# Block attention of the odd layer: as a stage after its input projection, or woven into it by quarter tiles

## The chip, the cores and the metric

The kernel runs on one core of one Trainium2 chip. The metric is the device time of one execution in microseconds (us); the runs of a kernel are summarised by their median. TensorE (PE in the rows, PEld its weight loads), VectorE (DVE), ScalarE (ACT), GpSimd (POOL) and SyncE (SP) each work through a queue of their own in order and wait for one another through semaphores.

## The reference: what is computed

One inference step of a two-layer decoder trunk for a prompt of 256 tokens and 8 samples of 8 new tokens (320 tokens in all, model width 2048, float32). Layer 0 mixes with a state-space scan and a short convolution, layer 1 with block-sparse attention; after each comes a cross-attention into 256 memory tokens, at the end a norm. The part at issue is layer 1:

```
q, k, v, g = split(rmsnorm(x) @ w_in)        # 16 q heads, 4 kv heads of 128, gate of 2048
prompt:  p = softmax(q.k * scale - slope * distance, causal);  o = p.v
sample:  past = 2048 tokens = 8 blocks of 256, in 16 pages of 128 tokens found by page_table
         gate = q . mean of a block's keys; the top 3 of 8 blocks, and the own new tokens, are kept
         p = softmax over the kept keys (with -slope * distance);  o = p.v
x = x + (o * silu(g)) @ w_out
```

## The kernel before

Activations lie transposed: 128 channels in the partitions, 320 tokens in the free dimension, 16 chunks `k`. A projection (`Proj`) is a list of output tiles of 128 channels. For each tile a weight block of 1 MB (`load`, issued on SP, rows of 512 bytes) is split into a rounded part (`high`, ScalarE, L120) and a rest (`low`, VectorE, L125), and `Proj.tile` issues 48 matmuls with 320 columns: per chunk the rounded weights with the rounded and the rest part of the activations (L164), then the rest weights (L168). Four weight buffers are loaded ahead (`RAW`), three rounded ones are kept (`HI`). Tiles rotate over four PSUM banks, or two where `banks=(0, 1)` is given.

`moba` runs layer 1's attention in stages, each closed by a barrier of all engines:
- the projection `p_od`: 40 tiles, 16 of q, 4 of k, 4 of v, 16 of the gate; VectorE evacuates each into `m_q`, `m_k`, `m_v`, `m_g`, ScalarE applies SiLU to the gate;
- six transposed copies of k and v (`m_krows`, `m_vrows`) that are stored;
- `prompt_attention`: per head scores (L1650), bias and maximum on VectorE, exponentials on ScalarE (L1686), turns (transposes on TensorE against an identity, L1672), values (L1663). The scores are computed for the whole 256 x 256 square;
- `moba_sample`: a hardware loop over 8 samples. SP loads 16 key pages per sample (256 KB, rows of 2 KB, address read from the page table with `value_load`), GpSimd the value pages (both L1861). TensorE turns each key page in 4 pieces (L1937) into two alternating banks, ScalarE copies them out (L2014). Then scores (L1943), biasing and block sums and maxima (L2053 to L2056), the ranking of blocks (a chain of small VectorE operations), nine exponentials (L2026), turns of the probabilities (L1956), values (L1970), a scaled output and its turn (L2001);
- `residual_block` for the output projection `p_odo`: it first splits the gated output into two parts (L2220, L2234) and then runs 16 tiles, adding each to the residual stream `xt`.

In the even layer another order exists already: the steps of its scan (such as L1027, L1039, L1047) stand between whole tiles of the projection `p_sc`.

Of the kernel before, what the change touches and what calls it, by code (L numbers as in the profile page):

```python
# [12 lines left out]
ds = bass.ds  # L13
# [33 lines left out]
def host_constants():  # L47
# [19 lines left out]
    head, tok = np.arange(128) // TS, np.arange(128) % TS  # L67
    past = (-slopes[head][:, None] * (PAST + tok[:, None] - np.arange(PAST)[None]).astype(f)).astype(f)
    col = np.arange(64)
    own = np.full((128, NB, 64), NEG, f)  # L70
    for b in range(NB):
        d = tok[:, None] - (col[None] - TS * b)
        ok = (col[None] // TS == b) & (d >= 0)
        own[:, b] = np.where(ok, -slopes[head][:, None] * d.astype(f), f(NEG))
# [3 lines left out]
    return {"c_main": c, "c_dist": dist, "c_past": past, "c_own": own.reshape(128, 512),  # L78
# [50 lines left out]
class Proj:  # L129
# [19 lines left out]
    def tile(self, pe, t, rhs, ready=None):  # L149
# [10 lines left out]
        for k in range(self.kch):  # L160
            if ready:
                ready(pe, k)
            for part in range(2):
                e.nc.tensor.matmul(out, hi[:, k, cols], rhs(k)[part], start=(k == 0 and part == 0), stop=False)  # L164
        if t % self.tps == 0:
# [3 lines left out]
        m.then_inc(e.pe_tile, 1)  # L169
# [1672 lines left out]
class Pages:  # L1842


    QUAD = 4

    def __init__(self, e, ctx):
        self.e = e
        self.s = ctx.enter_context(stage(e.nc, "pages", ["pages_in"] + [f"{k}_in{i}" for k in "kv" for i in range(NPG // self.QUAD)]))
        self.table = e.at("page_table", 82, [1, NB * NPG], I32)  # L1850
        self.krows = e.at("key_pages", 84, [128, NPG, 512])
        self.vrows = e.at("value_pages", 28, [128, NPG, 512])

    def load(self, eng, kind, b, g, free=None):

        src = self.e.d[f"cache_{kind}"][0].rearrange("n t h c -> n t (h c)")
        dst = self.krows if kind == "k" else self.vrows
        page = eng.value_load(self.table[0:1, ds(b * NPG + g, 1)], min_val=0, max_val=src.shape[0] - 1)
        if free:
            eng.wait_ge(*free)  # L1860
        eng.dma_start(dst[:, g:g + 1, :], src[ds(page, 1)].rearrange("n t c -> t n c")).then_inc(self.s[f"{kind}_in{g // self.QUAD}"], 16)  # L1861

    def first(self, sp):

        sp.dma_start(self.table[:], self.e.d["page_table"].rearrange("b n -> (b n)").unsqueeze(0)).then_inc(self.s["pages_in"], 16)
        sp.wait_ge(self.s["pages_in"], 16)
        for g in range(NPG):
            self.load(sp, "k", 0, g)


def moba_sample(e, pages, qt, kt_new, v_new, gt, nxt):

    nc, d = e.nc, e.d
    names = ["zeroed", "tables_in", "q_ready", "k_turned", "kt_out", "scores", "own_scores", "step", "biases",
             "exped", "recips", "p_turned", "pt_v", "pt_s", "v_used", "o_ready", "o_rows", "o_turned", "o_out"]
    QUAD, HALF = Pages.QUAD, NPG // 2
    with ExitStack() as ctx:
        s = ctx.enter_context(stage(nc, "ms", names))
        NP = PAST + TSA
        past, own = e.at("ms_past", 116, [128, PAST]), e.at("ms_own", 76.75, [128, NB, TSA])  # L1890
        krows, vrows = pages.krows, pages.vrows
        kt = e.at("ms_kt", 175, [128, KVH, PAST])
        p, pt = e.at("ms_p", 60, [128, NP]), e.at("ms_pt", 68.25, [128, (NPG + 1) * 128])
        orows = e.at("ms_orows", 78.75, [128, DH])
        above, tied = [e.at(f"ms_{n}", 79.25 + 0.25 * i, [128, NBLK, NBLK]) for i, n in enumerate(("above", "tied"))]
        qb = e.at("ms_q", 79.75, [128, AH, TS])
        gate, rank, drop, top, dropped, bias, den, nm, den1, rec = [
            e.at(f"ms_{n}", 80.25 + 0.0625 * i, [128, w]) for i, (n, w) in enumerate(
                (("gate", NBLK), ("rank", NBLK), ("drop", NBLK + 1), ("top", NBLK + 1), ("dropped", NBLK + 1), ("bias", NBLK + 1),
                 ("den", NBLK + 1), ("negmax", 1), ("den_sum", 1), ("rec", 1)))]  # L1900
        STEPS = 25
        with nc.Block() as block:
            @block.sync
            def _(sp):
                sp.dma_start(past[:], d["c_past"]).then_inc(s["tables_in"], 16)
                sp.dma_start(own[:], d["c_own"].rearrange("p (b t) -> p b t", b=NB)).then_inc(s["tables_in"], 16)
                with sp.Fori(0, NB - 1) as b:
                    for g in range(NPG):

                        pages.load(sp, "k", b + 1, g, (s["k_turned"], b * NPG + (NPG + g + 1)))  # L1910

                sp.wait_ge(s["v_used"], NPG + NB * NPG)
                for n in range(nxt.slot0, nxt.slot0 + RAW):
                    e.load(sp, n)

            @block.gpsimd
            def _(pool):
                with pool.Fori(0, NB) as b:
                    for g in range(NPG):

                        pages.load(pool, "v", b, g, (s["v_used"], b * NPG + (g + 1)))

            @block.tensor
            def _(pe):
                mm = nc.tensor.matmul
                pe.sem_inc(s["k_turned"], NPG)
                pe.sem_inc(s["v_used"], NPG)

                def turn(b, g):
                    if g % QUAD == 0:  # L1930

                        pe.wait_ge(pages.s[f"k_in{g // QUAD}"], b * 64 + 64)
                    if g >= 2 or not isinstance(b, int):

                        pe.wait_ge(s["kt_out"], b * NPG + (g - 1))
                    for h in range(KVH):
                        m = nc.tensor.transpose(e.bank[g % 2][:, 128 * h:128 * h + 128], krows[:, g, 128 * h:128 * h + 128], e.ident)  # L1937
                    m.then_inc(s["k_turned"], 1)

                def scores(b, q):  # L1940
                    pe.wait_ge(s["kt_out"], b * NPG + QUAD * (q + 1))
                    for h in range(KVH):
                        m = mm(e.bank[4 + q][32 * h:32 * h + 32, :], qb[:, 4 * h:4 * h + 4, :].rearrange("p g t -> p (g t)"),  # L1943
                               kt[:, h, 512 * q:512 * q + 512], start=True, stop=True)
                    m.then_inc(s["scores"], 1)

                def first_scores(b):
                    pe.wait_ge(s["q_ready"], b + 1)
                    scores(b, 0)
                    scores(b, 1)  # L1950

                def turn_probs(b, f):

                    pe.wait_ge(s["exped"], b * 9 + (2 * f + 3))
                    for a in range(4):
                        m = nc.tensor.transpose(e.bank[4 + f][:, 128 * a:128 * a + 128], p[:, 512 * f + 128 * a:512 * f + 128 * a + 128], e.ident)  # L1956
                    m.then_inc(s["p_turned"], 1)
                    if f == 0:
                        nc.tensor.transpose(e.bank[3][0:TSA, 0:128], p[:, PAST:NP], e.ident).then_inc(s["p_turned"], 1)

                def values(b, f):

                    if f < 3:
                        pe.wait_ge(s["pt_v"], b * 4 + (f + 2 if f else 1))
                    else:
                        pe.wait_ge(s["pt_s"], b + 1)
                    pe.wait_ge(pages.s[f"v_in{f}"], b * 64 + 64)
                    for g in range(QUAD * f, QUAD * f + QUAD):
                        for h in range(KVH):
                            m = mm(e.bank[2][32 * h:32 * h + 32, 128:256], pt[:, 128 * g + 32 * h:128 * g + 32 * h + 32],  # L1970
                                   vrows[:, g, 128 * h:128 * h + 128], start=g == 0, stop=False, skip_group_check=True)
                        m.then_inc(s["v_used"], 1)

                def batch(b, last):
                    for g in range(HALF, NPG):
                        turn(b, g)
                        if g % QUAD == QUAD - 1:
                            scores(b, g // QUAD)
                    for h in range(KVH):
# [3 lines left out]
                    if not last:  # L1983
                        for g in range(HALF):
                            turn(b + 1, g)
# [475 lines left out]
```

## Time and profile before

| what | us |
|---|---|
| median of 3 runs (lowest, highest) | 2281.72 (2277.15, 2282.34) |
| profiled execution, its own time | 2278.83 |
| span of the profile, first to last instruction | 2277.2 |
| TensorE busy | 2099.7 |
| VectorE busy | 1186.1 |
| ScalarE busy | 914.8 |

The profile is of one execution. Busy time counts instructions in flight; matmuls overlap, so the mean duration of one is longer than the distance from one to the next. The granted clock is TensorE's, as a share of full speed. "Idle before" is what an engine waited just ahead of an instruction, and behind the arrow stands what ended that wait.

### The profile page before, as it was taken

How to read it: one execution, taken by the hardware profiler on the slowest of the kernel's cores; microseconds unless marked ns; L12 is line 12 of the kernel's file. 1: busy time of each engine (PE TensorE's matmuls, PEld its weight loads, DVE VectorE, ACT ScalarE, POOL GpSimd, SP SyncE). 2: the span in 40 equal slices, each digit the busy share in tenths (PEclk: the TensorE clock that was granted, in tenths of full speed). 3: DMA queues.
4: the chain of work that ended last, by engine and by line, in shares of the span. 5: the costliest groups of instructions: out<-in, count | busy, mean ns of one | idle time of the engine just before them, and what ended most of it. 6: DMA issues, size and time to landing. Idle time of an engine off the chain costs nothing. (4 is left out here: it accounts for less than half of the span.)

```text
span 2277.2 us, 39583 instructions
## 1 busy us (share of the span) xinstructions
PE 2099.7 (92%) x15842; PEld 1972.9 (87%) x15842; DVE 1186.1 (52%) x1819; ACT 914.8 (40%) x1426; POOL 146.1 (6%) x247
## 2 busy tenths in 40 slices
PE   7999999999999999999999878999977878599976
PEld 6899999999999999999999868999965555499956
DVE  5658666464554644565454346333326555445335
ACT  7445544243342523454333234223325555333322
POOL 1010000101101010001000000000000333100000
PEclk9999999999999999999999989999989999799988
DMA  8585455655656556555555714555523998555711
GB/s 236 173 216 154 132 148 129 166 136 151 170 130 167 135 157 190 149 149 146 151 151 162 230 43 128 150 149 148 148 80 126 353 339 284 145 150 164 234 67 47
DMA packets 516776, 369.05 MB, mean 162 GB/s; under 512 B 10699, under 2 KB 469624, under 8 KB 515882
## 3 DMA queue, kind: packets, MB, share of 16 engines
q1 hardware_dynamic: 498498, 305.47, 47.8%
q0 software_dynamic: 18128, 61.43, 8.3%
q8 instruction: 113, 1.85, 0.3%
q14 instruction: 37, 0.30, 0.0%
HBM read 348.29 MB, written 18.57 MB: 161 GB/s over the span
## 5 line engine op out<-in xcount | busy, mean ns | idle before, releaser
L120 ACT ACTIVATE w_high<-w_raw 128x2048 fp32r<-128x2048 f32 x232 | 443.9, 1913 | 895.0 <-PE bank L168 827.6
L125 DVE TENSOR_TENSOR w_low<-w_raw,w_high 128x2048 fp32r<-128x2048 f32 x232 | 531.4, 2290 | 268.2 <-ACT w_high L120 268.0
L164 PE MATMUL bank<-x_hi,w_high 128*128 128x320 f32 x1664 | 495.1, 312 | 0.0
L164 PE MATMUL bank<-x_lo,w_high 128*128 128x320 f32 x1664 | 489.5, 309 | 0.0
L164 PEld LDWEIGHTS bank<-x_hi,w_high 128*128 128x128 f32 x1664 | 312.4, 188 | 1.1
L164 PEld LDWEIGHTS bank<-x_lo,w_high 128*128 128x128 f32 x1664 | 312.5, 188 | 0.2
L168 PE MATMUL bank<-x_hi,w_low 128*128 128x320 f32 x1664 | 260.9, 309 | 0.0
L168 PEld LDWEIGHTS bank<-x_hi,w_low 128*128 128x128 f32 x1664 | 248.3, 188 | 0.0
L164 PE MATMUL bank<-xo_x_hi,w_high 128*128 128x320 f32 x640 | 189.9, 311 | 8.3 <-PEq L102 8.3
L164 PE MATMUL bank<-xo_x_lo,w_high 128*128 128x320 f32 x640 | 189.4, 310 | 0.0
L164 PEld LDWEIGHTS bank<-xo_x_hi,w_high 128*128 128x128 f32 x640 | 121.1, 189 | 8.6 <-issue 8.5
L164 PEld LDWEIGHTS bank<-xo_x_lo,w_high 128*128 128x128 f32 x640 | 121.1, 189 | 0.1
L168 PE MATMUL bank<-xo_x_hi,w_low 128*128 128x320 f32 x640 | 100.4, 309 | 0.0
L2014 ACT ACTIVATE ms_kt<-bank 128x512 f32<-128x512 f32 x128 | 69.8, 595 | 73.2 <-PE bank L1937 73.1
L168 PEld LDWEIGHTS bank<-xo_x_hi,w_low 128*128 128x128 f32 x640 | 95.5, 188 | 0.0
L164 PE MATMUL bank<-m_o_hi,w_high 128*128 128x320 f32 x256 | 78.6, 321 | 15.4 <-DVE m_o_lo L2234 15.4
L1349 DVE TENSOR_TENSOR xt<-xt,bank 128x320 f32<-128x320 f32 x80 | 38.8, 485 | 103.1 <-PE bank L168 103.1
L1937 PEld LDWEIGHTS bank<-const,key_pages 128*128 128x128 f32 x512 | 55.7, 143 | 31.9 <-ACT ms_kt L2014 18.2
L1937 PE MATMUL bank<-const,key_pages 128*128 128x128 f32 x512 | 73.0, 287 | 11.0 <-ACT ms_kt L2014 8.6
L1861 POOL DMA_DIRECT2D value_pages<-in_cache_v x128 | 68.8, 538 | 197.7 <-issue 136.7
L164 PE MATMUL bank<-m_o_lo,w_high 128*128 128x320 f32 x256 | 78.1, 319 | 0.0
L164 PE MATMUL bank<-ysc_hi,w_high 128*128 128x320 f32 x256 | 76.3, 313 | 0.0
(417 smaller groups left out, 3511.5 us busy)
## 6 DMA issues: line engine op xcount, KB each, us to landing
w_raw<-in_ev_w_in SPq DMA_DIRECT2D x104, 1024.0 KB, 5.8
w_raw<-in_od_w_in SPq DMA_DIRECT2D x40, 1024.0 KB, 5.7
w_raw<-in_ev_w_out SPq DMA_DIRECT2D x32, 1024.0 KB, 5.8
key_pages<-in_cache_k SPq DMA_DIRECT2D x128, 256.0 KB, 4.6
value_pages<-in_cache_v POOLq DMA_DIRECT2D x128, 256.0 KB, 4.6
w_raw<-in_ca_w_kv SPq DMA_DIRECT2D x16, 1024.0 KB, 7.3
w_raw<-in_ca_w_q SPq DMA_DIRECT2D x16, 1024.0 KB, 5.6
w_raw<-in_od_w_out SPq DMA_DIRECT2D x16, 1024.0 KB, 5.9
```

Of the source, the lines that this page charges most:

```text
L120: self.nc.scalar.activation(self.w_high[n % HI][:], self.w_raw[n % RAW][:], ACT.Copy).then_inc(self.w_hi, 1)
L125: self.nc.vector.tensor_tensor(self.w_low[n % RAW][:], self.w_raw[n % RAW][:], self.w_high[n % HI][:].bitcast(F32), ALU.subtract).then_inc ...
L164: e.nc.tensor.matmul(out, hi[:, k, cols], rhs(k)[part], start=(k == 0 and part == 0), stop=False)
L168: m = e.nc.tensor.matmul(out, lo[:, k, cols], rhs(k)[0], start=False, stop=k == self.kch - 1)
L1349: e.nc.vector.tensor_tensor(e.xt[:, t, :], e.xt[:, t, :], p.bank(t)[:, 0:T], ALU.add).then_inc(e.bank_free, 1)
L1861: eng.dma_start(dst[:, g:g + 1, :], src[ds(page, 1)].rearrange("n t c -> t n c")).then_inc(self.s[f"{kind}_in{g // self.QUAD}"], 16)
L1937: m = nc.tensor.transpose(e.bank[g % 2][:, 128 * h:128 * h + 128], krows[:, g, 128 * h:128 * h + 128], e.ident)
L2014: nc.scalar.activation(kt[:, :, 128 * g:128 * g + 128], e.bank[g % 2][:].rearrange("p (h t) -> p h t", h=KVH), ACT.Copy).then_inc(s["kt_ou ...
```

## The change

The stages of layer 1 up to the output projection become one block without barriers (`moba_layer`, class `Moba`). `Proj.tile` becomes a generator `parts` that yields after each matmul. Each of the 40 tiles is cut into four quarters of 12 matmuls; `weave` puts the attention's steps of a quarter between equal runs of these matmuls. `steps(qr)` gives the steps of quarter `qr` from a written-out timetable, and ScalarE and VectorE go through the same timetable.

- The order of tiles is k0, k1, q0 to q7, v0, v1, k2, k3, q8 to q15, v2, v3, gate. Projections use banks 0 and 1; bank 2 holds sample scores, 3 to 5 are turn-over banks (`TN`), 6 sample outputs, 7 prompt scores.
- The samples are done in 8 units `U`, each of two samples and two kv heads, 12 quarters apart from quarter 40 on. A unit has four groups (`Q`, three quarters apart): key turns (`K`, two steps of 8 turns), scores (`S`) two quarters after, turns of probabilities (`T`) at 16 and values (`V`) at 19 quarters. A page DMA now moves half a page (two of the four kv heads: 128 rows of 1 KB, 128 KB), 512 of them instead of 256; two groups of pages fit into each ring. Indices are written out instead of computed in a loop.
- Probabilities lie in five chunks of 512 columns; the distance bias is made from one row of key numbers and a per-row slope, its constant part added to the block's bias.
- One prompt head goes with each tile of 11 to 18 and 23 to 30 (`pS`, `pT`, `pO`); its fully masked quarter is left out.
- The gate is `x * (1 + tanh(x/2)) / 2` instead of SiLU: a tanh on ScalarE and two operations on VectorE.
- New tiles lie where `xt` lay, so `xt` is written to DRAM at the start and read back at the end. The splits for the output projection begin during the last tiles.

```diff
-class Pages: ...
-def moba_sample(e, pages, qt, kt_new, v_new, gt, nxt): ...
-def moba(e, p_in, p_out, res_in): ...
+class Moba:
+    BASE0, PERIOD = 40, 12
+    SC, TN, MI, PR = 2, (3, 4, 5), 6, 7
+    TAIL, CHUNKS = 14, 5
...
+    def steps(self, qr):
+        j, qi = divmod(qr, 4)
+        if qi == 1 and j and 16 <= self.order[j - 1] < 24:
+            yield "rows", j - 1, 0
+        for U in self.rel(qr, 31):
+            yield "OT", U, 0
...
+            for U in self.rel(qr, 19 + 3 * a):
+                yield "V", U, a
...
+            for U in self.rel(qr, 16 + 3 * a):
+                yield "T", U, a
...
+            for U in self.rel(qr, 2 + 3 * a):
+                yield "S", U, a
...
+            for U in self.rel(qr, 3 * a):
+                yield "K", 4 * U + a, 0
+                yield "K", 4 * U + a, 1
+        if qi == 0:
+            for h in self.head(j - 1):
+                yield "pT", h, 0
+            for h in self.head(j):
+                yield "pS", h, 0
...
+    def page(self, eng, kind, Q, bi, free):
...
+        for g in range(4):
+            page = eng.value_load(self.table[0:1, ds(b * NPG + 4 * q + g, 1)], min_val=0, max_val=src.shape[0] - 1)
+            if g == 0 and free:
+                eng.wait_ge(*free)
+            eng.dma_start(dst[c % 4][:, g:g + 1, :], src[ds(page, 1), :, 256 * hp:256 * hp + 256].rearrange("n t c -> t n c")).then_inc(sem[c % 4], 16)
...
+    def sync(self, sp):
...
+            if qr % 4 == 0 and qr:
+                e.load(sp, m + qr // 4 - 1 + RAW)
...
+                if qr == self.BASE0 + 3 * Q + 1:
+                    for bi in range(2):
+                        self.page(sp, "k", Q + 2, bi, (s["turned"], self.fill[("K", Q, bi), 1] + 1))
...
+    def pool(self, pool):
...
+            for bi in range(2):
+                self.page(pool, "v", Q, bi, (s["v_used"], Q - 1) if Q >= 2 else None)
+        self.out_of(pool, ("OT", 7, 0))
+        pool.wait_ge(s["p_probs"], AH)
+        pool.dma_start(e.xt[:].rearrange("p c t -> p (c t)"), e.spill).then_inc(s["xt_in"], 16)
...
+    def turn_bank(self, pe, key, f=0):
+        i = self.fill[key, f]
+        if i >= 3:
+            pe.wait_ge(self.s["turn_out"], i - 2)
+        return self.e.bank[self.TN[i % 3]]
...
+    def gate_scalar(self, act, h):
...
+        e.nc.scalar.activation(self.th[h % 2][:], self.tb[h % 2][:], ACT.Tanh, scale=0.5).then_inc(s["tanh"], 1)
...
+def weave(pe, parts, steps, run):
+    count = 12 // (len(steps) + 1)
+    for step in steps:
+        for _ in range(count):
+            next(parts)
+        run(pe, step)
+    for _ in range(12 - count * len(steps)):
+        next(parts, None)
+
+def moba_layer(e, p_in, p_out, res_in):
...
+            for j in range(n):
+                parts = p_in.parts(pe, j, res_in.rhs, res_in.ready if j == 0 else None)
+                for qi in range(4):
+                    weave(pe, parts, list(b.steps(4 * j + qi)), b.tensor)
...
+                    if qi == 2:
+                        e.high(act, m + j + AHEAD)
...
+                    for step in b.steps(qr):
+                        b.scalar(act, step)
+                    for U in b.rel(qr, 13):
+                        b.exps(act, U)
...
-        p_od = Proj(e, columns(d["od_w_in"][0], wide(0, 40)))
-        p_odo = Proj(e, columns(d["od_w_out"][0], wide(0, 16)))
+        p_od = Proj(e, columns(d["od_w_in"][0], [128 * n for n in (16, 17, *range(8), 20, 21, 18, 19, *range(8, 16), 22, 23, *range(24, 40))]), banks=(0, 1))
+        p_odo = Proj(e, columns(d["od_w_out"][0], wide(0, 16)), banks=(0, 1))
...
-        res = moba(e, p_od, p_odo, res)
+        res = moba_layer(e, p_od, p_odo, res)
```

## Rows read from the trace of the kernel before

**Rows 1.** The page's busy times: engine, us, share of the span, instructions.

```profile
PE 2099.7 (92%) x15842; PEld 1972.9 (87%) x15842; DVE 1186.1 (52%) x1819; ACT 914.8 (40%) x1426; POOL 146.1 (6%) x247
```

**Rows 2.** Windows: stretch, length; PE, PEld, DVE, ACT, POOL busy; clock, DMA share, GB/s.

```profile
1395.60:1679.40 283.80, 283.80 (x1922) 283.50 (x1922) 108.72 (x79) 81.44 (x56) 0.00 (x0) 0.99 0.48 134
1679.40:1696.30 16.90, 2.93 (x25) 2.58 (x25) 2.56 (x4) 2.27 (x5) 2.56 (x4) 0.69 0.29 94
1696.30:1749.80 53.50, 41.66 (x192) 29.37 (x192) 39.43 (x96) 28.31 (x81) 0.00 (x0) 0.97 0.28 79
1749.80:1963.40 213.60, 170.15 (x2064) 113.47 (x2064) 107.71 (x273) 108.78 (x280) 68.82 (x128) 0.93 0.87 302
...
1779.00:1805.00 26.00, 21.26 (x262) 13.97 (x266) 13.43 (x35) 13.54 (x35) 9.01 (x17) 0.94 1.01 366
396.73:443.33 46.60, 46.60 (x385) 45.02 (x381) 22.87 (x41) 12.85 (x14) 7.52 (x10) 1.00 0.64 167
```

**Rows 3.** Timeline of layer 1: start us, us, instruction, idle before it.

```profile
1395.58 0.61 PE L164 MATMUL bank<-xo_x_hi,w_high 128*128 128x320 f32 x1 [8.29 <-PEq L102]
...
1975.88 0.60 PE L164 MATMUL bank<-m_o_hi,w_high 128*128 128x320 f32 x1 [12.89 <-DVE m_o_lo L2234]
...
1990.95 0.31 PE L164 MATMUL bank<-m_o_hi,w_high 128*128 128x320 f32 x1
```

**Rows 4.** Line L113, weight loads: plain tiles, woven even tiles; ns, first and last start.

```profile
L113 SPq DMA_DIRECT2D w_raw<-in_od_w_in x36: 367/367/367, 1404.5 to 1651.4; - x36
...
L113 SPq DMA_DIRECT2D w_raw<-in_ev_w_in x5: 368/368/368, 404.1 to 441.3; - x5
```

**Rows 5.** Timeline, merged runs of TensorE: sample stage, prompt stage, even layer.

```profile
1808.86 1.92 PE L1943 MATMUL bank<-ms_kt,ms_q 128*32 128x512 f32 x16
...
1823.31 0.91 PEld L1937 LDWEIGHTS bank<-const,key_pages 128*128 128x128 f32 x8 [0.44 <-ACT ms_kt L2014]
...
1828.02 0.81 PEld L1970 LDWEIGHTS bank<-value_pages,ms_pt 128*32 128x32 f32 x32 [0.17 <-DVE ms_pt L2093]
...
1711.64 1.03 PE L1650 MATMUL bank<-m_k,m_q 128*128 128x256 f32 x4
1712.50 1.11 PE L1663 MATMUL bank<-mp_pt,m_vrows 128*128 128x256 f32 x4
...
405.48 0.64 PE L1047 MATMUL bank<-scan_ce,s0t 128*64 128x8 f32 x16
```

**Rows 6.** Timeline, page issues: SP written out, POOL in its loop.

```profile
1698.55 17.32 SPq L1861 DMA_DIRECT2D key_pages<-in_cache_k  x16
...
1812.28 0.54 POOL L1861 DMA_DIRECT2D value_pages<-in_cache_v  x1 [0.74 <-issue]
```

**Rows 7.** Groups by line: count, busy us, mean ns, idle before and its releaser.

```profile
L120 ACT ACTIVATE w_high<-w_raw 128x2048 fp32r<-128x2048 f32 x232 | 443.9, 1913 | 895.0 <-PE bank L168 827.6
L125 DVE TENSOR_TENSOR w_low<-w_raw,w_high 128x2048 fp32r<-128x2048 f32 x232 | 531.4, 2290 | 268.2 <-ACT w_high L120 268.0
...
L2014 ACT ACTIVATE ms_kt<-bank 128x512 f32<-128x512 f32 x128 | 69.8, 595 | 73.2 <-PE bank L1937 73.1
L2026 ACT ACTIVATE ms_p<-ms_p,ms_bias 128x256 f32<-128x256 f32 x64 | 31.5, 497 | 0.0
...
L2053 DVE TENSOR_REDUCE ms_gate<-bank 128x2 f32<-128x512 f32 x32 | 22.0, 686 | 24.6 <-PE bank L1943 23.2 <-issue 1.4
```

**Rows 8.** DMA issues of the even layer: KB, median us to landing.

```profile
xt<-x_spill POOLq DMA_DIRECT2D x1, 2560.0 KB, 10.4
```

**Rows 9.** Timeline, a table load of ScalarE.

```profile
1696.29 1.28 ACT L1686 ACT_TABLE_LOAD   x1 [11.99 <-PEq L2325]
```

**Rows 10.** Groups of TensorE in the sample stage, 1750 to 1975, by form.

```profile
L1937 PE MATMUL bank<-const,key_pages 128*128 128x128 f32 x512 | 73.0, 287 | 11.0 <-ACT ms_kt L2014 8.6 <-PEq L1579 1.9 <-DMA key_pages<-in_cache_k 0.4
...
L1943 PE MATMUL bank<-ms_kt,ms_q 128*32 128x512 f32 x256 | 32.4, 601 | 11.0 <-ACT ms_kt L2014 11.0
L1956 PE MATMUL bank<-const,ms_p 128*128 128x128 f32 x128 | 25.6, 333 | 21.3 <-ACT ms_p L2026 21.3
```

More of the change, by code:

```diff
@@ L65, in host_constants @@
     dist = np.where(q >= k, (k - q).astype(f), f(NEG)).astype(f).reshape(128, 512)
-    head, tok = np.arange(128) // TS, np.arange(128) % TS
-    past = (-slopes[head][:, None] * (PAST + tok[:, None] - np.arange(PAST)[None]).astype(f)).astype(f)
-    col = np.arange(64)
[L70 to L74, printed above, removed]
+    row = np.arange(128)
+    bi, hi, g, tok = row // 64, row // 32 % 2, row % 32 // TS, row % TS
+    keys = np.broadcast_to(np.arange(BLK).astype(f)[None], (128, BLK))
+    unit = np.zeros((128, 18), f)
+    own = np.full((128, 8, 64), NEG, f)
+    col = np.arange(64)
+    for hp in range(2):
+        slope = slopes[8 * hp + 4 * hi + g]
+        unit[:, hp] = slope
+        unit[:, 2 + 8 * hp:10 + 8 * hp] = -slope[:, None] * (PAST + tok[:, None] - BLK * np.arange(NBLK)[None]).astype(f)
+        for bp in range(4):
+            b = 2 * bp + bi[:, None]
+            d = tok[:, None] - col[None] % TS
+            own[:, 4 * hp + bp] = np.where((col[None] // TS == b) & (d >= 0), -slope[:, None] * d.astype(f), f(NEG))
     qmask = np.broadcast_to((col[None] // TS == np.arange(NB)[:, None]).astype(f).reshape(1, 512), (128, 512))
@@ L168, in tile @@
             m = e.nc.tensor.matmul(out, lo[:, k, cols], rhs(k)[0], start=False, stop=k == self.kch - 1)
-        m.then_inc(e.pe_tile, 1)
+            if k == self.kch - 1:
+                m.then_inc(e.pe_tile, 1)
+            yield
+    def tile(self, pe, t, rhs, ready=None):
+        for _ in self.parts(pe, t, rhs, ready):
+            pass
     def done(self, eng, t):
@@ L1839, in _ @@
                     v.tensor_tensor(g, g, o[:, :, TS * (b % 4):TS * (b % 4) + TS], ALU.mult).then_inc(s["out"], 1)
[L1842 to L1868, printed above, removed]
@@ L2195, in cross_attention, with residual_block @@
     return res
-def residual_block(e, label, p, res, chunks, y, split, first=False):
+def residual_block(e, label, p, res, chunks, y, split):
     nc = e.nc
@@ L2333, in moba @@
-        moba_sample(e, pages, qt, kt, vrows[:, 2, :], gt, p_out)
-        pctx.close()
-    res = Residual(e, "odo", p_out, 124, VA_CROSS + KC)
-    residual_block(e, "odo", p_out, res, KC, lambda c: gt[:, c, :], split, first=True)
+                            b.evacuate(dve, j - 1)
+                    for U in b.rel(qr, 1):
+                        b.gather(dve, U)
+                    for U in b.rel(qr, 30):
+                        b.unit_out(dve, U)
+                    for U in b.rel(qr, 20):
+                        b.inverse(dve, U)
@@ new lines, in _ @@
+                    if qi == 2:
+                        for h in b.head(j):
+                            b.prompt_normed(dve, h)
+                    for step in b.steps(qr):
+                        if step[0] == "S":
+                            b.scored(dve, step[1], step[2])
+                        if step[0] == "pS":
+                            b.prompt_scored(dve, step[1])
+                    for U in b.rel(qr, 11):
+                        b.biases(dve, U)
+                    if qi == 3:
+                        e.low(dve, m + j + AHEAD)
+                        if j > 24:
+                            b.gate_vector(dve, j - 25)
+                        if j >= 36:
+                            for h in range(3 * (j - 36), 3 * (j - 35)):
+                                b.split_vector(dve, h, h + 1)
```

786 lines of the change are left out of this document (498 added, 288 removed).

## The prediction

> **What bounds the kernel now.** I read the busy shares first: TensorE is busy for 92% of the span [rows 1], so only a stage in which it is not busy can give much back. The windows by stage find it [rows 2]. In the input projection of the odd layer (1395.6 to 1679.4) TensorE is busy for all of its 283.8 us at clock 0.99, while the DMA engines are at 0.48. Then the roles change: the stretch that turns and stores the key and value rows has TensorE busy for 2.9 of 16.9 us, the prompt attention for 41.7 of 53.5, and the sample attention for 170.2 of 213.6 with the DMA engines at 0.87. So matrix work without transfers is followed by transfers with little matrix work. From the first matmul of the projection (1395.58) to the first of the output projection (1975.88) are 580.3 us [rows 3]; the first output tile then lasts until 1990.95, 15.1 us. What a plain tile costs, I take from the weight loads, which go out once per tile: 35 steps between 1404.5 and 1651.4, 7.05 us each [rows 4]. So that first tile is 8.0 us over, and **588.3 us** is what the change can work on; the rest of the program is left as it is.
>
> **The change part by part.** It puts the attention's TensorE work between the projection's matmuls. The projection's own 283.8 us stay. What goes is the time in which TensorE waits; what comes are the attention's instructions at their plain price, the switches between the two kinds, and new waits. One "group" below is four key pages each for two sequences and two heads (32 groups; three quarter tiles apart).
>
> *Attention instructions.* Eight turns of keys keep the weight port for 0.91 us, 0.114 each; 32 value instructions take 0.81; two score steps 1.92; a 256-column half pass of the prompt 0.215 (four from 1711.64 to 1712.50) [rows 5]. A group has 16 key turns (1.82), one score step (0.96), 4 turns of probabilities (0.46), 32 value instructions (0.81), and a quarter of each unit's small steps (0.2, estimated from those prices): 4.2 us. A prompt head now leaves out the masked quarter: three half-pass equivalents for the scores, three for the values (1.29) and 3 turns (0.34): 1.6. Each of eight row turnings has 3: 0.34.
>
> *Switches.* The even layer weaves its scan between tiles already. There five loads go out from 404.1 to 441.3, 9.30 us apart [rows 4], 2.25 over a plain tile, for 4 turns and 8 equal matmuls (12 x 0.114) and 16 small ones (0.64 less their tail of 0.2) [rows 5]: 1.8. The other 0.45 goes to four switches: 0.11 each. The new order has about six steps to a group with projection matmuls on both sides, 12 switches, 1.3 us; a head 0.7, a row step 0.2. I take these, since that row is the nearest; the bounds are nothing, and twice as much (0.22).
>
> So a group costs 5.5 us, a head 2.3, a row step 0.55: 32 x 5.5 + 16 x 2.3 + 8 x 0.55 = 217, and 501 with the projection.
>
> *What has to stay hidden.* A group lasts three quarter tiles plus its own work: 5.3 + 5.5 = 10.8 us. Against that:
> - Issue. Pages are now halves, so 8 issues per group and queue. SP's written-out loop took 17.32 us for 16 (1.1 each), the pool's rolled loop 0.54 + 0.74 = 1.28 each [rows 6]: 8.8 to 10.2 us, and SP also has 0.75 weight loads of 0.37 [rows 4]. It fits, with little room. Two groups of pages are held, so a page has some 21 us from its issue to its use. On SP's queue a page issue that waits for its group's key turns stands before the next weight load; weights are held four tiles deep, so a late one is felt three tiles on. The pool's key-row stores come before its first pages, long before these are used.
> - Transfer. A group brings 2.1 MB of pages and 0.79 MB of weights. Weights in 512-byte rows reach 134 GB/s at share 0.48, so some 279 when full; whole page rows of 2 KB reach 366 at 1.01 [rows 2]. Half rows between these: 5.7 to 7.5 us, with weights 8.6 to 10.3. Hidden at either end. If a half row costs an engine what a whole row costs (the outer bound), pages take 11.5 and the group 14.3: not hidden.
> - ScalarE: 4 key copies and a probability copy of 0.595, 0.75 of a weight rounding of 1.91, some 1.5 of exponentials (eight of 0.50 and a small one to a unit, with their sums): 5.9 of 10.8 us, and about 2 more per tile with a head. VectorE: three passes of 0.69, 0.75 of 2.29, ranking and evacuation about 1.3: 5.1 [rows 7]. Both are covered, but each works in order, so a copy can queue behind a rounding or nine exponentials.
> - The residual stream is spilled, and read back (10.4 us [rows 8]) after the last unit; five quarter tiles, the splits and a whole output tile lie before its use. Uncovered it would cost 10.4 at most.
>
> *Tanh for SiLU.* A table load is 1.28 us [rows 9]. No row shows tanh beside exp. From tile 25 on both are used, some 16 changes: 0 to 20 us, on ScalarE alone, some 2.6 us per tile, which is inside the slack above; so zero on the path. The Trainium skill (ScalarE: Activation LUTs, Table sets) puts tanh into exp's set; by it there is no such load, and no row shows either.
>
> *New waits.* A step that waits holds TensorE's queue: behind it stand the rest of its tile, then VectorE's evacuation of that tile, and the next page and weight issues. Two row steps at the start wait for the norm's scale: 2. Per unit (eight) the nine exponentials and a rounding stand before the next key copies: about 1 each, an estimate. Sum 10; bounds 0, and what TensorE waits for ScalarE now in the sample stage: 8.6 + 11.0 + 21.3 = 41 [rows 10].
>
> *The end.* After the last tile come an evacuation, a tanh, two gate products, a split: TensorE waits for about 4.5 us, and a first output tile at a lower clock adds some 3 of the old 8.0.
>
> **Sum:** 501 + 10 + 7.5 = 518.5 against 588.3, a gain of 70. The profiled execution took 2278.8 us (span 2277.2), so 2209; the runs' median of 2281.7 is 2.9 above it: **2210 us** in round numbers.
>
> One rule speaks against this sum. The granted clock in the sample stage is 0.93, but in the woven tiles of the even layer it is 1.00, with TensorE never idle [rows 2]. The Trainium skill (TensorE: Matmul & The Clock Gate, Part 4: PE-mode transpose) says that transposes don't count as activity for that clock. By it a stretch with up to 16 turns in a quarter could fall to the lower level; the trace agrees with it only so far as the stages rich in turns are below 1. It is rival E.
>
> **The rivals.**
> - *B, switches and waits cost next to nothing.* For it: turns run on without a gap in the trace. Then a group costs 4.3, a head 1.7, a row step 0.4, no waits, 4.5 at the end: 283.8 + 168 + 4.5 = 456, gain 132: 2150.
> - *C, the waits move along.* All 41 us on ScalarE and not 10: 2241; with twice the switches' price for part of the groups, 2255. For it: the copy of turned keys holds up TensorE by 0.2 us and more at each pair even now; three banks instead of two speak against it.
> - *D, half rows cost whole rows.* The engines then set 14.3 us per group, 458 for 32. This takes the place of the 24 tiles under them (169), the groups (176), the heads (37) and most waits (8): 390. That is 68 more: 2278, no gain. Against it: the 512-byte rows reach 279 GB/s.
> - *E, the other sign.* The clock falls in the woven stretch because steps leave TensorE without projection work. The lower level is half of the upper. The gain of 70 is gone once 70 us of the stretch's 390 run at that level; a third of it would give 2340. Against it: the even layer's 1.00.
>
> **How the numbers follow.** A difference of 0.3% (7 us) is about what this kernel's runs can tell from none. Chances: the forecast, 2175 to 2240, 0.52; B 0.23; C 0.15; D 0.05; E 0.05. Faster takes the first three, 0.90; D counts mostly as the same, 0.03; slower 0.07. The range 2150 to 2255 reaches from B to C.
>
> **What would show it.** One stretch of about 500 us from the first projection matmul to the first output matmul in place of 580; TensorE busy throughout; key-page transfers at 10 to 11 us per group, DMA share 0.8 to 0.9, clock 1.00. Plain tiles outside the woven stretch stay at 7.05. Wrong would be: TensorE waits of over 1 us per group by ScalarE's copies (C); waits on page transfers (D); a clock well under 1 (E); gaps of 0.03 us at switches (B).

## The result

The changed kernel takes 2193.64 us (median of 4 runs, 2192.21 to 2195.12) against 2281.17 for the kernel before on the same chip: ratio 0.962, 95% interval 0.960 to 0.964. The gain is 87.5 us where 70 were forecast. The profiled execution took 2193.05 us.

The page's busy times, after (answers to [rows 1]):

```profile
PE 2069.1 (94%) x15826; PEld 1954.3 (89%) x15826; DVE 1173.7 (54%) x1856; ACT 928.8 (42%) x1503; POOL 222.1 (10%) x386
```

The timeline of TensorE after, at the first matmul of the projection, at the first of the output projection and at that of its second tile (answers to [rows 3]):

```profile
1398.83 0.61 PE L170 MATMUL bank<-xo_x_hi,w_high 128*128 128x320 f32 x1 [8.28 <-PEq L108]
...
1900.17 0.43 PE L170 MATMUL bank<-m_o_hi,w_high 128*128 128x320 f32 x1 [4.11 <-DVE m_o_lo L2381]
...
1908.82 0.31 PE L170 MATMUL bank<-m_o_hi,w_high 128*128 128x320 f32 x1
```

The stretch that was 580.3 us is 501.3, and the first output tile, which was 15.1, is 8.65. Those two are 79.0 + 6.4 = 85.4 of the 85.8 us between the two profiled executions.

The windows of the whole stretch and of two of its tiles without a prompt head (tiles 20 and 21; columns as in [rows 2]):

```profile
1398.83:1900.17 501.34, 475.36 (x4186) 417.41 (x4187) 254.70 (x504) 243.42 (x515) 147.36 (x272) 0.99 0.77 231
...
1619.12:1646.42 27.30, 27.30 (x281) 22.27 (x279) 9.62 (x16) 10.52 (x17) 10.75 (x20) 1.00 0.84 255
```

TensorE is never idle in those two tiles, at clock 1.00. Over two plain tiles (14.1) they carry 13.2 us of attention in 8 quarters, that is 8/3 groups: 4.95 us a group, where the prediction had 5.5. What is left of waiting in the stretch (the view of waits: TensorE's line, what it waited for, us in total, times, longest):

```profile
PE bank L2176 <- ACT m_q L2309: 10.9, 6, 2.9
...
PE bank L2220 <- DMA value_pages<-in_cache_v: 7.6, 2, 4.2
PE bank L170 <- DVE m_o_lo L2381: 4.1, 1, 4.1
PE bank L2167 <- DVE m_k L2406: 1.8, 2, 1.2
PE bank L2176 <- ACT past_keys L2284: 1.2, 1, 1.2
```

L2176 turns keys, L2284 is ScalarE's copy of them, L2220 the value step, L2309 ScalarE's copy of a prompt head's output, L2167 the turning of key rows. Inside the stretch that is 21.5 us, where 10 were forecast; 4.1 more stand at its end.

**What a step costs.** The timeline of TensorE after, a value step, a score step and a key step between projection matmuls:

```profile
1619.26 0.31 PE L170 MATMUL bank<-xo_x_lo,w_high 128*128 128x320 f32 x1
1619.50 1.08 PE L2220 MATMUL bank<-value_pages,ms_pt 128*32 128x128 f32 x32
1620.51 0.41 PE L170 MATMUL bank<-xo_x_hi,w_high 128*128 128x320 f32 x1
1620.77 0.31 PE L170 MATMUL bank<-xo_x_lo,w_high 128*128 128x320 f32 x1
...
1623.91 0.31 PE L170 MATMUL bank<-xo_x_lo,w_high 128*128 128x320 f32 x1
1624.15 1.06 PE L2195 MATMUL bank<-past_keys,ms_q 128*32 128x512 f32 x8
1625.15 0.42 PE L170 MATMUL bank<-xo_x_hi,w_high 128*128 128x320 f32 x1
1625.40 0.31 PE L170 MATMUL bank<-xo_x_lo,w_high 128*128 128x320 f32 x1
...
1626.57 0.31 PE L170 MATMUL bank<-xo_x_lo,w_high 128*128 128x320 f32 x1
1626.71 1.04 PE L2176 MATMUL bank<-const,key_pages 128*128 128x128 f32 x8
1627.51 0.39 PE L170 MATMUL bank<-xo_x_hi,w_high 128*128 128x320 f32 x1
1627.74 0.31 PE L170 MATMUL bank<-xo_x_lo,w_high 128*128 128x320 f32 x1
```

Read from the matmul ahead of a step to the second one behind it (the first alone hides part of the price: the distance to the second is 0.23 to 0.26 and not 0.15), and take off two plain distances of 7.05/48 = 0.147 [rows 4]. The key step: 1.17 - 0.29 = 0.88, or 0.110 for each of 8 turns, which is their plain price [rows 5]: its two switches cost nothing. The score step: 1.49 - 0.29 = 1.20 against the prediction's 0.96, 0.24 over. The value step: 1.51 - 0.29 = 1.22 against its 0.81, 0.4 over. These two are on tiles of 32 columns. Both plain prices are rough (0.81 is the time of the weight port alone); e3 below gives the price of a break without them, 0.33.

Medians over all steps, read so: 0.88 (64 key steps), 0.44 (4 turns of probabilities), 0.33 (3 turns, of a head or of rows), 0.11 (1 turn), 0.65 for either pair of a prompt head's matmuls; 1.20 and 1.21 for scores and values, 0.45 and 0.55 for those of a unit's own tokens.

The Trainium skill (TensorEngine Tiling (Array Packing), Key Properties) says that a change of tiling mode drains TensorE, a change of tile alone does not. The steps on 32-column tiles agree, by 0.24 and 0.4; the one turn with 64 columns shows no price (0.11).

### The profile page after: what moved, and what is told of

It is laid out like the page before. It is cut to its first block and busy times, and to the rows that moved or that the text cites. A ratio compares the mean times of both kernels' runs of the same rounds, so it can differ in the third digit from the quotient of the medians.

```text
span 2191.4 us, 40334 instructions
## 1 busy us (share of the span) xinstructions
PE 2069.1 (94%) x15826; PEld 1954.3 (89%) x15826; DVE 1173.7 (54%) x1856; ACT 928.8 (42%) x1503; POOL 222.1 (10%) x386
## 5 line engine op out<-in xcount | busy, mean ns | idle before, releaser
L131 DVE TENSOR_TENSOR w_low<-w_raw,w_high 128x2048 fp32r<-128x2048 f32 x232 | 531.2, 2290 | 283.7 <-ACT w_high L126 283.5
L170 PE MATMUL bank<-xo_x_hi,w_high 128*128 128x320 f32 x640 | 206.0, 332 | 8.3 <-PEq L108 8.3
L170 PE MATMUL bank<-xo_x_lo,w_high 128*128 128x320 f32 x640 | 196.4, 318 | 0.0
L2098 POOL DMA_DIRECT2D value_pages<-in_cache_v x256 | 137.8, 538 | 222.0 <-issue 148.3
L175 PE MATMUL bank<-xo_x_hi,w_low 128*128 128x320 f32 x640 | 117.3, 321 | 0.0
L2284 ACT ACTIVATE past_keys<-bank 128x512 f32<-128x512 f32 x128 | 67.9, 593 | 56.7 <-PE bank L2176 56.0
L2176 PE MATMUL bank<-const,key_pages 128*128 128x128 f32 x512 | 68.1, 275 | 12.5 <-ACT m_q L2309 10.9
L170 PE MATMUL bank<-y_hi,w_high 128*128 128x320 f32 x256 | 75.3, 309 | 0.0
```

What stands on the lines that cost most here:

```text
L131: self.nc.vector.tensor_tensor(self.w_low[n % RAW][:], self.w_raw[n % RAW][:], self.w_high[n % HI][:].bitcast(F32), ALU.subtract).then_inc ...
L2098: eng.dma_start(dst[c % 4][:, g:g + 1, :], src[ds(page, 1), :, 256 * hp:256 * hp + 256].rearrange("n t c -> t n c")).then_inc(sem[c % 4], 16)
L2176: t = nc.tensor.transpose(bank[:, 128 * g:128 * g + 128], self.kring[c % 4][:, g, 128 * hi:128 * hi + 128], e.ident)
L2284: f(self.kt_past[:, 2 * bi + hi, :], b[:], ACT.Copy).then_inc(s["turn_out"], 1)
```

## The experiments

Each was timed in 5 rounds (e10 in 3) against the kernel before on the same chip; the chips differ between groups of runs, so the ratios are what is compared. "Stretch" is, in the profiled execution alone, from the first matmul of the projection to the first of the output projection. In the code, "..." marks what is left out.

| run | us | ratio (95% interval) | stretch |
|---|---|---|---|
| ref_after | 2194.57 | 0.9633 (0.9620 to 0.9646) | 502.2 |
| e1_bunched | 2199.79 | 0.9653 (0.9640 to 0.9666) | 508.7 |
| e2_split_keys | 2197.90 | 0.9645 (0.9632 to 0.9658) | 502.6 |
| e3_split_values | 2200.76 | 0.9657 (0.9644 to 0.9671) | 506.9 |
| e4_two_banks | 2210.94 | 0.9700 (0.9685 to 0.9715) | 514.9 |
| e5_silu_gate | 2204.39 | 0.9672 (0.9658 to 0.9686) | 511.7 |
| e6_high_last | 2197.68 | 0.9645 (0.9629 to 0.9660) | 505.2 |
| e7_both | 2194.01 | 0.9627 (0.9612 to 0.9642) | 497.2 |
| e8_thirds | 2191.27 | 0.9616 (0.9602 to 0.9629) | 494.3 |
| e9_spread_all | 2175.05 | 0.9552 (0.9539 to 0.9565) | 480.3 |
| e10_after_projection | 2356.19 | 1.0340 (1.0324 to 1.0356) | 662.5 |
| e11_merged | 2173.28 | 0.9534 (0.9521 to 0.9547) | 480.5 |

**The changed kernel again.** 

> The changed kernel itself, on the same chip as the next three. All theories: 2193.6 us, 0.962 of the kernel before; the other three are read against it.

 It came out so.

**Steps bunched.**

```diff
-    count = 12 // (len(steps) + 1)
+    count = 0
```

> All steps of a quarter are issued first and its 12 projection matmuls behind them, so that a group has about 6 switches and not 12. Switch theory (my prediction: 0.11 us at each switch): 32 x 6 x 0.11 = 21 us are saved, and waits for copies of turned keys come, since four half steps follow one another on three banks: some 0.9 us per group, 29 in all; 2202. Rival (a switch to or from turns is free, only the steps on 32-column tiles pay 0.1 to 0.3 us): next to nothing is saved and the waits come: 2215 to 2225. If even spreading is worth nothing: 2194 or less.

Slower by 5 us (the intervals overlap; the stretch by 6.5). The forecast sign was right, the parts were not: a run of 16 turns takes 1.67 us from first to last turn at 19 of the 32 groups, 0.109 each with one step of 0.145, so three banks are enough there; only at the other 13, where ScalarE has exponentials or a rounding in hand, do the turns wait. The waits inside the stretch grow by 7 us, next to nothing is saved. So even spreading is worth some 6 us, not 20 to 30.

**Key steps cut in two**, one step of 4 turns for each of the two kv heads:

```diff
-            for hi in range(2):
+            for hi in range(2) if half is None else (half,):
...
-                    weave(pe, parts, list(b.steps(4 * j + qi)), b.tensor)
+                    steps = []
+                    for step in b.steps(4 * j + qi):
+                        steps += [(step, 0), (step, 1)] if step[0] == "K" else [(step, None)]
+                    weave(pe, parts, steps, lambda pe, x: b.tensor(pe, *x))
```

> Each key step of 8 turns is cut into two of 4, with projection matmuls between: 64 more breaks, 128 more switches. Switch theory: 128 x 0.11 = +14 us, less what the copies no longer hold up (0 to 11): 2197 to 2208. Rival (turns switch for free; in the changed kernel a step of 8 turns takes 0.79 us between projection matmuls and one of 4 takes 0.36): 64 x (2 x 0.36 - 0.79) = -4.5 us, and less again by what the copies hold up: 2180 to 2189.

The time alone does not decide: 2197.90 is 3.3 us over the reference with overlapping intervals, and stands at the lower end of the switch theory's range, which let up to 11 us of waits for copies go. The profiled execution does: the waits at key turns did not go (15.1 us against 12.2), and 128 more switches cost 0.4 us of stretch where 0.11 each would be 14. So the switch theory falls for turns. The timeline of it, one cut step:

```profile
1628.77 0.31 PE L170 MATMUL bank<-xo_x_lo,w_high 128*128 128x320 f32 x1
1628.91 0.60 PE L2176 MATMUL bank<-const,key_pages 128*128 128x128 f32 x4
1629.27 0.39 PE L170 MATMUL bank<-xo_x_hi,w_high 128*128 128x320 f32 x1
1629.50 0.31 PE L170 MATMUL bank<-xo_x_lo,w_high 128*128 128x320 f32 x1
```

1629.50 - 1628.77 - 0.29 = 0.44, half of 0.88. The rival's -4.5 us was wrong too: its 0.36 and 0.79 were read only up to the first matmul behind the step.

**Value steps cut in two**, in the same way (two of the four value pages in each half):

```diff
-                for g in range(4):
+                for g in range(4) if half is None else range(2 * half, 2 * half + 2):
...
```

> Each value step of 32 matmuls on 32-column tiles is cut into two of 16, with a projection matmul or more between: 32 more breaks, 64 more switches. Switch theory: 64 x 0.11 = +7 us: 2201. Rival (column-tiled steps alone pay, 0.29 us for a value step): 32 x 0.29 = +9 us: 2203. If no switch costs anything: 2194. Together with the cut key steps it tells where the price of a switch sits: the switch theory has both slower, the rival the keys faster and the values slower.

Slower by 6.2 us (the intervals just touch), the stretch by 4.6. The time fits both theories; the timeline, one half step, gives the price of a break:

```profile
1622.11 0.31 PE L170 MATMUL bank<-xo_x_lo,w_high 128*128 128x320 f32 x1
1622.35 0.64 PE L2220 MATMUL bank<-value_pages,ms_pt 128*32 128x128 f32 x16
1622.92 0.41 PE L170 MATMUL bank<-xo_x_hi,w_high 128*128 128x320 f32 x1
1623.17 0.31 PE L170 MATMUL bank<-xo_x_lo,w_high 128*128 128x320 f32 x1
```

A half takes 1623.17 - 1622.11 - 0.29 = 0.77, two of them 1.54 against 1.21: 0.33 for a break, where two switches of 0.11 would be 0.22 and the rival said 0.29; 10.6 us over 32. (16 matmuls more add 1.21 - 0.77 = 0.44, so 32 cost 0.88 without a break, and not 0.81.) The last values' wait on their pages, 7.8 in the reference, is 4.0 here and gives 3.8 back; some 2 us more of the 10.6 are missing from the stretch, and no run accounts for them in full. Keys free, values not: the price sits at the steps on 32-column tiles.

**Two turn-over banks.**

```diff
-    SC, TN, MI, PR = 2, (3, 4, 5), 6, 7
+    SC, TN, MI, PR = 2, (3, 4), 6, 7
-        if i >= 3:
-            pe.wait_ge(self.s["turn_out"], i - 2)
+        if i >= 2:
+            pe.wait_ge(self.s["turn_out"], i - 1)
```

> Two turn-over banks in place of three; bank 5 stays unused. If the third bank is what hides ScalarE's copies (mine): each second key step of a group waits 0.3 to 0.6 us for a copy, 10 to 20 us over 32 groups, and the waits behind the copy of a prompt head's output grow by some 6: 2210 to 2222. Rival (even spreading alone leaves the copies time enough): 2194 to 2198.

15 to 16 us slower, the stretch by 12.7: the third bank is worth that. The place was right only in part: the waits at key turns grow from 12.2 to 21.0 us, but at the crowded tiles and not at each second step, and the median key step is still 0.88. The turns of prompt probabilities rise from a median of 0.33 to 0.42, the slowest to 0.60. Its view of waits:

```profile
PE bank L2176 <- ACT m_q L2309: 15.2, 6, 3.5
...
PE bank L2176 <- ACT past_keys L2284: 4.1, 5, 1.8
```

**SiLU for the gate.**

```diff
-        e.nc.scalar.activation(self.th[h % 2][:], self.tb[h % 2][:], ACT.Tanh, scale=0.5).then_inc(s["tanh"], 1)
+        e.nc.scalar.activation(self.th[h % 2][:], self.tb[h % 2][:], ACT.Silu).then_inc(s["tanh"], 1)
...
-        v.scalar_tensor_tensor(x[:, 0:n], t[:, 0:n], 1.0, x[:, 0:n], ALU.add, ALU.mult).then_inc(s["swish"], 1)
+        v.scalar_tensor_tensor(x[:, 0:n], t[:, 0:n], 0.0, t[:, 0:n], ALU.add, ALU.max).then_inc(s["swish"], 1)
...
```

> The gate by SiLU on ScalarE with as many operations as before (VectorE's first product becomes a copy). SiLU stands beside exponentials in tiles 25 to 30 and at the units' exponentials in tiles 31 and 34: 16 table loads of 1.28 us, 20 us more on ScalarE. Mine (ScalarE has slack, so the tanh costs and gives nothing): 2194 to 2200, with no wait of TensorE at a gate. Rival (the loads stand before copies that TensorE waits for): up to 20 us, 2205 to 2215. If tanh itself loads tables beside exp, the loads are there in both and the time is 2194.

9 to 10 us slower, just short of the rival's range. ScalarE's groups show the 16 loads (gate, prompt exponentials, sample exponentials), where the changed kernel has one in all of the attention:

```profile
L2334 ACT ACT_TABLE_LOAD x8 | 10.3, 1283 | 0.1
L2325 ACT ACT_TABLE_LOAD x6 | 7.7, 1283 | 0.1
L2317 ACT ACT_TABLE_LOAD x2 | 2.6, 1283 | 0.0
```

The wait behind a prompt head's output rises from 11.0 to 16.6 us:

```profile
PE bank L2176 <- ACT m_q L2309: 16.6, 6, 4.4
```

So ScalarE's slack does not hide them all: 15 loads more, 19.2 us, cost 9 to 10. Only 3.5 of these are waits inside the stretch (the one for value pages is shorter here). The rest can be laid to the clock: behind the longer waits it stands at its lower level, 0.50 (1.2 GHz), for 20.5 us of the stretch after its start, against 6.8 in the reference; that can cost half of the difference, 6.8. The Trainium skill (ScalarE: Activation LUTs, Table sets) puts tanh into exp's set; with tanh no load stands at the gate, and the trace agrees.

**What those six waits are.** ScalarE's timeline in the changed kernel before the longest of them, and TensorE's at its end:

```profile
1753.41 0.49 ACT L2317 ACTIVATE ms_p<-ms_p,ms_bias 128x256 f32<-128x256 f32 x1
...
1753.90 0.46 ACT L2334 ACTIVATE m_tanh<-m_gate 128x320 f32<-128x320 f32 x1
1754.26 1.90 ACT L126 ACTIVATE w_high<-w_raw 128x2048 fp32r<-128x2048 f32 x1
1756.06 0.36 ACT L2309 ACTIVATE m_q<-bank 128x256 f32<-128x256 f32 x1
```

```profile
1756.57 1.53 PE L2176 MATMUL bank<-const,key_pages 128*128 128x128 f32 x8 [2.92 <-ACT m_q L2309]
1757.75 1.41 PE L175 MATMUL bank<-xo_x_hi,w_low 128*128 128x320 f32 x4
```

The ninth exponential, a tanh and a whole rounding stand ahead of the copy; the key turns wait for its bank. The other five, and the wait behind L2284, are alike: nine exponentials and a rounding stand ahead of the copy in ScalarE's timeline each time, in some of them without the tanh. Four runs follow this up, two of them together with the wait for value pages.

**The rounding behind the copies.**

> In the third quarter of a tile ScalarE does the copies of that quarter first and the rounding of weights (1.9 us) behind them. Theory (the 10.9 us for which key turns wait behind the copy of a prompt head's output are the rounding that stands before that copy in ScalarE's queue): they go, 2184. Rival (three banks are too few whatever the order): 2194. If the late rounding makes the projection wait for weights instead: over 2194, with waits on the rounded weights.

```diff
-                    if qi == 2:
-                        e.high(act, m + j + AHEAD)
...
                     for step in b.steps(qr):
                         b.scalar(act, step)
+                    if qi == 2:
+                        e.high(act, m + j + AHEAD)
```

Not faster (stretch +3.0). The wait behind L2309 falls to 1.7 us, and that behind the copies of keys rises from 1.2 to 10.7:

```profile
PE bank L2176 <- ACT past_keys L2284: 10.7, 9, 1.6
...
PE bank L2176 <- ACT m_q L2309: 1.7, 3, 1.1
```

ScalarE's timeline shows why: the rounding now stands between that copy and the next ones.

```profile
1757.60 0.36 ACT L2309 ACTIVATE m_q<-bank 128x256 f32<-128x256 f32 x1
1757.86 1.90 ACT L126 ACTIVATE w_high<-w_raw 128x2048 fp32r<-128x2048 f32 x1
1759.66 2.26 ACT L2284 ACTIVATE past_keys<-bank 128x512 f32<-128x512 f32 x4
```

**Beside that, the last value pages on two queues.**

> As the kernel with the rounding behind the copies, and beside that the value pages of the second sequence of the last four groups are issued by SP, whose key pages are all out by then, and not by GpSimd. Theory (the 7.6 us for which the last value steps wait come from GpSimd's issue, 1.16 us a page and back to back at the end): both waits go, 2176. Rival (the pages' transfers are what is late): 2184, as without it.

```diff
+            for Q in range(28, 32):
+                if qr == self.BASE0 + 3 * Q + 14:
+                    self.page(sp, "v", Q, 1, (s["v_used"], Q - 1))
...
-            for bi in range(2):
+            for bi in range(2 if Q < 28 else 1):
...
```

The late rounding stays in, so 2176 was not to be had; against e6 the stretch is 8.0 us shorter (the median 3.7, with overlapping intervals), and the wait for value pages falls from 7.5 to 0.9 with the same transfers. Issue was the cause, not the transfer.

**The rounding in thirds**, without e7's change (`high_part`, left out here, rounds one third).

> The rounding of a weight block in three pieces of 704, 704 and 640 columns, one behind the copies of each of the first three quarters. Theory (what TensorE waits for is the longest piece of ScalarE work that stands before a copy: nine exponentials, 4.4 us, and then 1.9 us of rounding; with the rounding moved whole the wait only moved): of the 11.0 us behind a prompt head's output about 1.2 us go at each of six places, and nothing comes elsewhere: 2187 to 2190. Rival (ScalarE's sum of work in the crowded tiles is what counts, and three pieces add 0.4 us a tile): 2194 to 2198, the waits standing at other copies.

```diff
-                        e.high(act, m + j + AHEAD)
+                    if qi < 3:
+                        e.high_part(act, m + j + AHEAD, qi)
```

Median 3 us better than the reference, within the intervals; the stretch 7.9 shorter. The wait behind L2309 goes from 11.0 to 4.3, while 1.8 come at the copies of keys, and the value pages' falls from 7.8 to 3.7, which this change was not meant to touch: the length of a piece counts, but with nine exponentials still in one the theory holds in part only.

**Everything in pieces**: the thirds of e8, the pages of e7 and the exponentials three by three.

> Three things: the rounding in three pieces, the nine exponentials of a unit in three quarters (3 and 3 and 3) instead of one, and the last value pages of the second sequence issued by SP. Theory: all waits behind ScalarE's long pieces go (11.0 + 1.2) and the 7 us for the last value pages: 2174 to 2178, faster than the changed kernel. Rival (the waits move along, as with the late rounding): 2186 to 2190, only the pages' 7 us.

```diff
...
-                    for U in b.rel(qr, 13):
-                        b.exps(act, U)
+                    for at, ks in ((13, (NBLK, 0, 1)), (14, (2, 3, 4)), (15, (5, 6, 7))):
+                        for U in b.rel(qr, at):
+                            b.exps(act, U, ks)
```

2175.05, as the theory had it, and faster than the changed kernel (0.9552 against 0.9633). Of the waits inside the stretch 3.8 us are left, and the clock of the stretch is 1.00. Its waits and its window:

```profile
PE bank L2185 <- DVE m_k L2427: 2.9, 2, 2.3
PE bank L2194 <- ACT past_keys L2305: 0.9, 1, 0.9
```

```profile
1398.45:1878.76 480.31, 472.07 (x4186) 414.75 (x4187) 256.09 (x504) 251.08 (x595) 138.64 (x256) 1.00 0.80 241
```

ScalarE does more here (251.1 us against 243.4), and TensorE's waits behind it fall from 12.2 us in the reference to 0.9: it was the length of what stands ahead of a copy, not the sum. The stretch is 21.9 us shorter than the reference's: 18.1 are waits, 7.8 of these for value pages, and up to 3.4 the clock, which no longer falls behind them (next section).

**The samples behind the projection.** The timetable is moved from quarter 40 to 160; the gate's last product and the splits follow the last unit.

```diff
-    BASE0, PERIOD = 40, 12
+    BASE0, PERIOD, NJ = 160, 12, 69
...
-            for j in range(n):
+            for j in range(b.NJ):
...
```

> The same steps, banks and half pages, but the eight units of sample attention come in quarters behind the 40 tiles, without projection matmuls between; prompt heads stay woven. Theory (weaving hides the issue of 8 half pages per group, 1.16 us each on GpSimd, and the latencies): 283.8 + 30 with the heads, and 32 groups of 9.3 us issue: 610 to 640 in place of 502, 2300 to 2330, slower than the kernel before. Rival (the gain is the rewritten attention, TensorE's 157 us and some waits, wherever it stands): 530 to 550, 2222 to 2240.

Slower than the kernel before by 3.4%; the rival falls. The size was 26 us beyond the theory's upper end. GpSimd's page issues (ns of one: least, median, most; first and last start) and TensorE's waits in it:

```profile
L2098 POOL DMA_DIRECT2D value_pages<-in_cache_v x240: 537/537/551, 1764.7 to 2051.2; - x120
```

```profile
PE bank L2176 <- DMA key_pages<-in_cache_k: 65.8, 31, 3.9
PE bank L2220 <- DMA value_pages<-in_cache_v: 62.1, 15, 6.8
```

240 issues in 286.5 us are 1.20 each, 9.6 a group, with the DMA engines at 0.76 in 1800 to 1900. The first value step comes at 1762.0, 49 us after the first key step (1713.1), since 19 quarters lie between and GpSimd holds two groups only; this lead the theory had left out. The half pages stay in this run, so it does not show what whole pages behind the projection would take. The Trainium skill (DMA: Bandwidth & Descriptors, Issuing engines are not separate DMA queues) calls the time of starting a transfer usually small beside the transfer; here, at 128 KB a transfer (3.0 us from issue to landing, 1.20 from issue to issue), it sets the pace.

**Fewer breaks**, on top of e9: a unit's own scores and own values follow its last long step at once.

```diff
+                        if step[0] in "SV" and step[2] == 4:
+                            steps[-1] = [*steps[-1], step]
...
```

> As e9_spread_all, but the two short column-tiled steps of a unit (scores and values of its own new tokens) follow their long ones without a projection matmul between: 16 breaks fewer, all of them at column-tiled steps. Theory (a break costs 0.2 to 0.35 us there and nothing at turns): 8 x (0.35 + 0.20) = 4.4 us less, the stretch 476 in place of 480.3, 2171. Prediction's price (0.11 a switch, two to a break): 16 x 0.22 = 3.5 us, 476.8. If breaks at column-tiled steps cost nothing after all: 480, 2175.

Inconclusive as a time (2173.28, intervals overlap; stretch 480.5). By the reading above the scores with the own ones take 1.30 in place of 1.20 + 0.45, the values 1.56 in place of 1.21 + 0.55: 0.35 and 0.20 less, 8 x 0.55 = 4.4 us, as expected. In the profiled execution the first three tiles of the projection are 2.4 us slower (0.6 of it a longer wait) and the other waits 1.6 us more, which takes it back. So no time shows the gain.

## Why the prediction was right, and where it was off

The mechanism was right: the stretch is the projection, the attention's instructions and a remainder of waits. The sum against the changed kernel's profile:

| term | predicted | measured |
|---|---|---|
| projection | 283.8 | 283.5 |
| 32 groups | 176 (5.5) | 157.4 (4.92) |
| 16 heads | 37 (2.3) | 26.4 (1.65) |
| 8 row steps | 4.4 (0.55) | 2.6 (0.33) |
| waits | 10 | 21.5 |
| what is left | no term | 5.8 |
| end | 4.5 | 4.1 |
| first output tile, over plain | 3 | 1.6 |
| sum | 518.5 | 502.9 |

The group is 2 x 0.88 + 1.20 + 0.44 + 1.21 and 0.31 for a quarter of a unit's small steps; the 283.5 are 40 plain tiles of 7.04 and 1.9 for a first tile at the lower clock. Groups, heads and row steps are the medians above times their number; the 5.8 are a remainder, not a reading. The forecast missed the time by 16 us because 31 too many for the attention and 17 too few for waits and what comes with them partly cancel; that it missed by no more is luck.

- **Instructions**: right. The prices from the stages before (4.2 a group, 1.6 a head, 0.34 a row step) against 4.92, 1.65 and 0.33, the first with its switches.
- **Switches**: the step that failed. "0.11 each", from one row of the even layer, was given to all. Turns and the prompt's matmuls switch for nothing (e2); steps on 32-column tiles pay 0.24 to 0.4 by the reading above, 0.33 a break by e3. A group pays some 0.7 and not 1.3, a head nothing and not 0.7: 31 us too much in all. The row of the even layer has no step on 32-column tiles at all: beside its turns there are 16 matmuls on 64-column tiles [rows 5] and these on 64-row tiles:

```profile
404.40 1.16 PE L1039 MATMUL bank<-b_masked,scan_xd 64*128 64x128 f32 x8
```

  What a change to or from 64-row tiles costs, no run shows. Rival B had their prices nearer (168 in place of 186), but no waits.
- **Waits**: mis-sized the other way, 21.5 for 10, inside the bounds. The nine exponentials and a rounding that stand before the next key copies were the mechanism for 12.1 of them, at seven places, and e6, e8 and e9 show it; "about 1 each", 8 in all, was too little. The two row steps came as forecast, 1.8 for 2. The other large one, value pages at the end, was not foreseen as one: the issue "fits, with little room" is right for tiles with attention in each quarter (10.2 us a group there against 8 issues of 1.15, 9.2) and wrong where TensorE has less to do and GpSimd's order runs back to back (e7).
- **What follows a wait** had no term. Behind the wait of 2.92 us above, eight turns take 1.18 to the next matmul instead of 0.80, and the granted clock is 0.67 in the 1.5 us there:

```profile
1756.50:1758.00 1.50, 1.43 (x9) 1.46 (x10) 1.50 (x1) 1.38 (x3) 0.00 (x0) 0.67 0.14 57
```

  After its start the stretch has two pieces at the lower level (clock 0.50), 6.8 us together: from 1757.01, behind that wait, and from 1873.06, behind the one of 4.2 us for value pages. That can cost 3.4 of the 5.8. In e9 no such piece is left, and the same sum leaves 2.8. These show in eleven key steps of 1.07 to 1.17 us in place of 0.88: one turn in each starts late, 0.25 to 0.41 us behind the matmul before it, which the view of waits does not count while that matmul is in flight. That they are short waits for a bank is likely, but not shown.
- **Tanh at zero**: right for tanh. The reason given, that slack would hide loads, was wrong: e5 pays half of them.
- **Rivals**: C, the waits moved along, is seen in small. D did not come: DMA share 0.84 with TensorE never idle. Nor did E: 0.99 in the stretch, falling only behind waits; in e1 the clock is 1.00 over a run of 16 turns (1632.5 to 1634.2).
- **Cover**: with the samples' attention behind the projection the same steps are 3.4% slower than the kernel before (e10). The gain is in the weaving; half pages with one issue each need the cover.

## What to carry to other kernels

Price a woven step by kind: here full-array turns cost their plain time between other matmuls, and a break at steps on 32-column tiles cost 0.2 to 0.35 us (e3, e11), so cut the former as one likes and keep the latter together. What TensorE then waits for is the longest single piece of work that an in-order engine has ahead of a copy, and here the waits of 2.9 and 4.2 us cost more than themselves, since the clock fell behind them; cut that piece (e9) and do not just move it (e6). Many small transfers belong under work that hides their issue, and the queue that issues them should be checked where that work thins out.

## What was not expected of the hardware

- A page issue on GpSimd, written out with its address read, takes 1.15 to 1.2 us, of which the instruction is 0.54 (e10); that of SP 1.12 (33 in 36.93 us).
- A rounding of 2048 columns takes 1.91 us, its three pieces 0.77 on average, 2.3 together (e9): 0.4 us a tile for cutting, all of it hidden.
